# Fifteen residual transposes and six gate transposes of a two-block hybrid network moved from TensorE to the sync engine's DMA transpose

## The reference

```python
def hybrid_layer(x, norm_g, w_in, ...):
    u = rms_norm(x, norm_g)
    p = u @ w_in
    qk, v, o, z_a, ig, fg, xb, z_b = jnp.split(p, SPLIT_AT, axis=-1)
    ...
    xc = causal_dwconv(xb, lru_conv_w) + lru_conv_b
    y_b = rg_lru(xc.astype(f32), w_a, b_a, w_x, b_x, lam).astype(x.dtype) * jax.nn.silu(z_b)
    return x + jnp.concatenate([y_a, y_b], axis=-1) @ w_out

# second stack, each of four layers
        h = rms_norm_2(x, norm_g[i])
        z = h @ w_in
        ...
        branch = jnp.concatenate([mix_out, mem_out], axis=-1) * jax.nn.silu(gate)
        x = x + branch @ w_out[i]
```

## Time and profile before

| | us |
|---|---|
| runs of the kernel | 3285.24, 3285.38, 3286.81 (median 3285.38) |
| the profiled execution's own time | 3287.08 |
| its span | 3285.3 |
| PE busy | 3274.6 (100% of the span) |
| DVE busy | 2085.7 (63%) |
| ACT busy | 1748.3 (53%) |
| DMA engines' mean share | 58.1% for the load queue |

### The profile page before, as it was taken

One profiled execution on the slowest core, in us unless ns is written; L12 is line 12 of the kernel. 1 busy time (PEld: TensorE's weight loads), 2 busy tenths in 40 slices (PEclk: granted clock), 3 DMA queues, 4 the chain that ended last, 5 costly groups with the idle time before them and its releaser, 6 DMA issues.

```text
span 3285.3 us, 39697 instructions
## 1 busy us (share of the span) xinstructions
PE 3274.6 (100%) x15310; PEld 2728.1 (83%) x15310; DVE 2085.7 (63%) x2843; ACT 1748.3 (53%) x2322; POOL 173.9 (5%) x241
## 2 busy tenths in 40 slices
PE   9999999999999999999999999999999999999999
PEld 7888888888888888888888888888888888888887
DVE  6557655756757755657667665665565677757564
ACT  5554555546654455546655564455544555545563
POOL 2000000000000000000000000000000322200000
PEclk9999999999999999999999999999999999999999
DMA  8665666565565566565567665566656566665565
GB/s 273 211 200 172 207 190 188 192 191 175 182 185 179 187 198 194 185 200 174 184 197 223 186 209 181 170 178 187 193 181 190 168 181 180 193 207 186 183 199 173
DMA packets 352060, 626.77 MB, mean 191 GB/s; under 512 B 58428, under 2 KB 60804, under 8 KB 351488
## 3 DMA queue, kind: packets, MB, share of 16 engines
q1 hardware_dynamic: 339248, 590.49, 58.1%
q0 software_dynamic: 10336, 27.45, 2.7%
q10 hardware_dynamic: 2288, 6.30, 0.5%
HBM read 608.10 MB, written 6.62 MB: 187 GB/s over the span
## 4 chain that ended last, share of the span: by engine, by line
PE 98%; DVE 1%; DMA 0%; ACT 0%; issue 0%; SPq 0%; ACTq 0%
PE acc L1697 30%; PE acc L1699 30%; PE acc L1698 30%; PE tr L1784 1%; PE nm L1887 1%; PE tr L1766 1%; PE tr L1697 0%; PE tr L1699 0%; PE tr L1875 0%; PE tr L1698 0%; PE sc L1861 0%; DMA weights_raw<-in_w_mem_kv_dram 0%; PE sc L1852 0%; DVE weights_lo L1249 0%; PE tr L1887 0%; PE sc L1866 0%
## 5 line engine op out<-in xcount | busy, mean ns | idle before, releaser
L1249 DVE TENSOR_TENSOR weights_lo<-weights_raw,weights_hi 128x1024 fp32r<-128x1024 f32 x1103 | 1343.9, 1230 | 922.7 <-ACT weights_hi L933 918.7
L933 ACT ACTIVATE weights_hi<-weights_raw 128x1024 fp32r<-128x1024 f32 x1103 | 1160.5, 1058 | 1079.0 <-PE acc L1699 1034.0
L1697 PE MATMUL acc<-weights_hi,u_hi 128*128 128x512 f32 x3136 | 1238.2, 395 | 0.0
L1699 PE MATMUL acc<-weights_hi,u_lo 128*128 128x512 f32 x3136 | 1222.8, 390 | 0.0
L1698 PE MATMUL acc<-weights_lo,u_hi 128*128 128x512 f32 x3136 | 1221.6, 390 | 0.0
L1697 PEld LDWEIGHTS acc<-weights_hi,u_hi 128*128 128x128 f32 x3136 | 589.2, 188 | 123.8 <-issue 4.3
L1699 PEld LDWEIGHTS acc<-weights_hi,u_lo 128*128 128x128 f32 x3136 | 588.9, 188 | 123.6
L1698 PEld LDWEIGHTS acc<-weights_lo,u_hi 128*128 128x128 f32 x3136 | 589.4, 188 | 119.1
L1697 PE MATMUL acc<-weights_hi,y_hi 128*128 128x512 f32 x1280 | 502.6, 393 | 1.3 <-DVE y_lo L1253 1.2
L1699 PE MATMUL acc<-weights_hi,y_lo 128*128 128x512 f32 x1280 | 498.7, 390 | 0.0
L1698 PE MATMUL acc<-weights_lo,y_hi 128*128 128x512 f32 x1280 | 498.2, 389 | 0.0
(11 more groups left out here) (279 smaller groups left out, 1931.3 us busy)
## 6 DMA issues: line engine op xcount, KB each, us to landing
weights_raw<-in_w_in_dram SPq DMA_DIRECT2D x384, 512.0 KB, 3.7
weights_raw<-in_w_out_dram SPq DMA_DIRECT2D x256, 512.0 KB, 4.4
weights_raw<-in_a_w_in_dram SPq DMA_DIRECT2D x176, 512.0 KB, 4.2
weights_raw<-in_b_w_in_dram SPq DMA_DIRECT2D x112, 512.0 KB, 3.7
weights_raw<-in_c_w_in_dram SPq DMA_DIRECT2D x112, 512.0 KB, 4.3
weights_raw<-in_w_mem_kv_dram SPq DMA_DIRECT2D x63, 512.0 KB, 4.8
kv_scratch<-work ACTq DMA_DIRECT2D x8, 512.0 KB, 5.4
qk_tiles<-in_w_a_dram POOLq DMA_DIRECT2D x8, 512.0 KB, 4.4
```

Of the source, the lines that this page charges most:

```text
L933: SC_E.activation(WH[:, b % RING], RAW[:, b % RING], ACT.Copy).then_inc(sem("hi_done"), 1)
L1249: V.tensor_tensor(WL[:, b % RING], RAW[:, b % RING], WH[:, b % RING].bitcast(F32), ALU.subtract).then_inc(sem("lo_done"), 1)
L1697: T.matmul(dst, hi_l, hi_r, start=start, stop=False, **kw)
L1699: return T.matmul(dst, lo_l, hi_r, start=False, stop=stop, **kw)
```

## The change

Three edits and what goes with them.

First, in all five layer ends the tiles of columns 0 to 1535 (`x0`, `x1`, `x2`) go through `xbar`, and only `x3` stays with `tp`. The buffers are `u0` and `u1` in `work`; `x2` uses `u0` again and has its `join` four slots after `apart`, not five.

Second, in both hybrid layers the gate tile of groups p = 0, 1, 2 goes through `apart`, a `turn` and a new piece `zjoin` (ACT, two instructions), and `lrz` reads it from SBUF. `lrz` and `lry` stand three slots later than before. Group 3 keeps `cz`.

Third, every `xbar` now has its low part on DVE as a piece of its own, `low`, two slots after `join`. `apart` on a buffer waits for that `low`. One of the gMLP tiles gets a buffer of its own, `a0`.

```diff
-ISSUE, JOIN = 8, 5
+ISSUE, JOIN, LOW = 8, 5, 2
...
-    def xbar(slot, src, ready, dst, kt0, gain, buf):
+    def xbar(slot, src, ready, dst, kt0, gain, buf, join=JOIN):
 
         q = apart(slot, src, ready, buf)
-        return pl.piece(slot + JOIN, "join", dst=dst, kt0=kt0, gain=gain, at=q, buf=buf)
+        p = pl.piece(slot + join, "join", dst=dst, kt0=kt0, gain=gain, at=q, buf=buf)
+        pl.piece(slot + join + LOW, "low", at=p, buf=buf)
+        return p
...
         def lru_gate(p):
             zb = pl.chunk(("w_in", l, COL_ZB + CH * p, 0), "tok", "u", "zb")
-            pl.piece(pl.here() + 3, "cz", at=zb)
-            pl.piece(pl.here() + 5, "lrz", l=l, p=p)
-            lr.append(pl.piece(pl.here() + 7, "lry", l=l, p=p))
+            if p == 3:
+                pl.piece(pl.here() + 3, "cz", at=zb)
+                pl.piece(pl.here() + 5, "lrz", l=l, p=p)
+                lr.append(pl.piece(pl.here() + 7, "lry", l=l, p=p))
+            else:
+                q = apart(pl.here() + 1, "xt", ("zb_out", zb), "z")
+                pl.piece(pl.here() + 6, "zjoin", at=q, buf="z")
+                pl.piece(pl.here() + 8, "lrz", l=l, p=p, at=q)
+                lr.append(pl.piece(pl.here() + 10, "lry", l=l, p=p))
...
-            xt.append(tp(o + 1, "x%d" % j, ("ox_out", ox), "u", 4 * j,
-                         ("par2", FGN + 4 * j, 1) if l else ("par", NPAR + NG + 4 * j, 1)))
+            gain = ("par2", FGN + 4 * j, 1) if l else ("par", NPAR + NG + 4 * j, 1)
+            xt.append(tp(o + 1, "x3", ("ox_out", ox), "u", 12, gain) if j == 3 else
+                      xbar(o + 1, "x%d" % j, ("ox_out", ox), "u", 4 * j, gain, "u%d" % (j % 2), 4 if j == 2 else JOIN))
...
+                    elif k == "zjoin":
+                        act.wait_ge(sem("half_t_z"), 16 * (p.at.nth + 1))
+                        for t in range(2):
+                            to = joined("z")[:, :, P * t:P * t + P].bitcast(U16).rearrange("p f (k s) -> p s f k", s=2)
+                            i = SC_E.activation(to, turned("z")[:, 8 * t:8 * t + 8].rearrange("p (s f) k -> p s f k", s=2),
+                                                ACT.Copy)
+                        i.then_inc(sem("zj_out"), 1)
...
-                    elif k == "join":
+                    elif k == "low":
+                        p = p.at
                         hi, lo = ACTS[p.dst]
```

More of the change, by code:

```diff
@@ L453, in make_plan @@
                 ts.append(tp(pl.here() + 4, "o", ("sv_out", sv), "y", 8, None) if grp == 2 else
-                          xbar(pl.here() + 4, "o", ("sv_out", sv), "y", 4 * grp, None, "a"))
+                          xbar(pl.here() + 4, "o", ("sv_out", sv), "y", 4 * grp, None, "a" if grp else "a0"))
         else:
@@ L493, in make_plan @@
                 pl.piece(o, "sq", j=j, ready=("ox_out", ox))
-                xt.append(tp(o + 1, "x%d" % j, ("ox_out", ox), "u", 4 * j,
-                             ("par2", NG2 + 16 * (i + 1) + 4 * j, 1)))
+                gain = ("par2", NG2 + 16 * (i + 1) + 4 * j, 1)
+                xt.append(tp(o + 1, "x3", ("ox_out", ox), "u", 12, gain) if j == 3 else
+                          xbar(o + 1, "x%d" % j, ("ox_out", ox), "u", 4 * j, gain, "u%d" % (j % 2), 4 if j == 2 else JOIN))
     return pl.close()
@@ L890, in _ @@
                         wait(pool, "ox_out", p.last.get("ox"))
+                        wait(pool, "jn_lo", p.last.get("low"))
                         pool.dma_start(WS, A["a_w_s_2"][p.a].rearrange("h t s -> t h s")).then_inc(sem("ws_in"), 16)
@@ L982, in _ @@
                             act.wait_ge(sem("half_t_" + p.buf), 16 * p.nth)
-                        if p.buf == "q":
+                        if p.buf == "z":
+                            wait(act, "tp_pe", last["tp"])
+                            wait(act, "half_in", last["apart"])
+                            wait(act, "lrz_y", last.get("lrz"))
+                            wait(act, "mo_out", last["mo"])
+                        elif p.buf == "q":
                             wait(act, "mo_out", last.get("mo"))
@@ L987, in _ @@
                         else:
-                            wait(act, "jn_lo", last.get(("join", p.buf)))
+                            wait(act, "jn_lo", last.get(("low", p.buf)))
                         for t in range(2):
@@ L1076, in _ @@
                         wait(act, "cz_pe", last.get("cz"))
+                        wait(act, "half_in", last.get("apart"))
                         for t in range(2):
@@ L1174, in _ @@
                         SC_E.activation(SQB, SQB, ACT.Sqrt).then_inc(sem("lr_sq"), 1)
+                    elif k == "zjoin":
[5 more added lines that the diff above has]
+                        i.then_inc(sem("zj_out"), 1)
                     elif k == "lrz":
-                        wait(act, "cz_pe", p)
+                        if p.at:
+                            wait(act, "zj_out", last["zjoin"])
+                        else:
+                            wait(act, "cz_pe", last["cz"])
                         wait(act, "lw_pe", last["lgate"])
@@ L1179, in _ @@
                         for j in range(2):
-                            i = tanh(ZT[:, 2 * j:2 * j + 2], TR[:, j].rearrange("p (a b) -> p a b", b=256), scale=0.5)
+                            z = joined("z")[:, 2 * j:2 * j + 2] if p.at else TR[:, j].rearrange("p (a b) -> p a b", b=256)
+                            i = tanh(ZT[:, 2 * j:2 * j + 2], z, scale=0.5)
                         i.then_inc(sem("lrz_t"), 1)
@@ L1537, in _ @@
                             z = ZT[:, 2 * j:2 * j + 2]
[L1538 removed]
+                            raw = joined("z")[:, 2 * j:2 * j + 2] if p.at else TR[:, j].rearrange("p (a b) -> p a b", b=256)
+                            i = stt(z, z, 1.0, raw, ALU.add, ALU.mult)
                         step(i)
@@ L1562, in _ @@
                         wait(dve, "tp_pe", last["tp"])
+                        wait(dve, "half_in", last["apart"])
                         cs = slice(CH * p.j, CH * p.j + CH)
```

4 lines of the change are left out of this document (2 added, 2 removed).

## The result

The changed kernel takes 3320.25 us (median of 4 runs, 3316.20 to 3322.17); the kernel before, run beside it, 3285.68 (3285.24 to 3286.81). The ratio is 1.0103, with a 95% interval of 1.0090 to 1.0115: 34.6 us slower, where 38.5 were forecast. The profiled execution took 3321.58 us; its span, from the first to the last instruction, is 3319.8.

A forecast was written before the change was run, and what follows sets the result against it. PE, busy 3274.6 of 3285.3 us, was taken as the bound; 22.4 + 2.6 + 13.5 = 38.5 us slower, with PE's 18.9 given back inside it, made 3324 us, range 3290 to 3345.

The forecast's parts named there:

- PE gives back 0.90 us a group: On PE's list: 21 groups of eight transposes fewer, 0.90 us each, 18.9 us in all.
- Separate low parts at nothing: Low parts two slots later on DVE and buffer `a0`: zero, with +-2 us in all.
- ACT's rounding put behind `apart`, and its block late by 1.7: Recurrent groups 1 and 2: `apart` delays block 533's rounding, so PE waits 1.7 us to start that block.
- Group 0, two instances, 1.3 us each: Recurrent group 0: landing hidden, gate products 1.2 to 1.3 us later each, 2.6 us in all.
- Groups 1 and 2, four instances, 5.6 us each: Recurrent groups 1 and 2: late landing and the chain behind it end each instance 5.6 us later, 22.4 us.
- the landing: SP's transposes: landing 6.7 us after issue (5.4 to 8.3), with ACT waiting 3.0 us at `zjoin`.
- The 17.1 us of DVE's chain: Recurrent groups: from `lrz`'s tanh through DVE's list and convolution to PE's gate products takes 17.1 us.
- Layer ends, five, 2.7 us each: Layer ends: PE waits 0.3, 2.8 and 2.4 us against 2.7 given back; 2.7 net each, 13.5 us.
- SP's list: A transpose holds SP's list 4.60 us; later loads cost nothing, 0.5 us each place as upper end.
- (a): Rival: PE's relief stands alone, ACT and DVE catch up, no remainder late; 3266.5 us, chance 0.15 (or most of it).
- (b): Rival: only recurrent groups are late, layer ends hide all and gain 13.5 us; 3297 us, chance 0.10.
- (c): Rival: a transpose lands like a load, 4.4 us; 3303 us, chance 0.08 shared with a mild form of both waits.

The follow-up runs named there:

- e3: Changed kernel with all layer-end and gate tiles put back on PE, leaving only separate low parts and buffer `a0`: 3285.45 us.
- e11: Changed kernel, gate groups back on PE, transposes of `u0` and `u1` issued one slot earlier, `x3`'s transposes on PE one slot later: 3273.88 us.
- e1: Changed kernel with the recurrent gate groups put back on PE, layer ends left changed: 3295.5 us.
- e4: Changed kernel with gate groups back on PE and only `x0` and `x1` by SP, `x2` and `x3` on PE: 3285.73 us.
- e2: Changed kernel with all layer-end tiles put back on PE, gate tiles of groups 0 to 2 still by SP: 3312.1 us.
- e9: e2 with `warm(12)`, small matmuls nothing reads, on PE before the gate products: 3307.17 us.
- e12: e11 with the `join` of `x2` one slot later, five after its `apart`: 3275.28 us.
- e7: e2 with 24 calls of a small matmul nothing reads on PE before the gate products: 3322.62 us.
- e8: e2 without three quarters of the low part in `lry` for groups 0 to 2, so `y_lo` is incomplete: 3304.56 us.

## Why the prediction was right, and where it was not

The total came out near, and part of that is luck. By the traces, the mechanism as the prediction stated it costs 2.4 us in group 0, 19.0 in groups 1 and 2 and 4.5 at the layer ends, 25.9 in place of 38.5. The six stretches of half clock, which it had at nothing, add 9.4, and the one in the trace before takes off 1.7; of the 0.9 that is left to the 34.5 between the two spans, 0.6 is at the start of the kernel. Terms that were too large and one that was missing nearly cancelled.

**PE gives back 0.90 us a group: right**, within what can be read: 0.85 by the busy times of e3 and e11.

**Separate low parts at nothing: right.** e3, within 0.1% of none. The gate read from SBUF costs nothing either: the three products of `lrz` take 2.47 us (1623.98 to 1626.45), where they took 2.46.

**ACT's rounding put behind `apart`, and its block late by 1.7: right.** The rows have 1.55 of waiting.

**Group 0, two instances, 1.3 us each: right, but for the clock.** By PE's block starts, one against the other in the traces before and after, the instances cost 1.2 and 2.8. The second has the half clock behind its stop and the first hasn't; without its 1.6 it is 1.2 too.

**Groups 1 and 2, four instances, 5.6 us each: the sum is right by two errors.** The traces have 5.9, 5.8, 7.2 and 6.3, 25.2 in all against 22.4. 1.5 to 1.6 of each is half clock (four of four), so the stated chain cost 4.3, 4.3, 5.7 and 4.7. The step that was mis-sized is the landing: 6.7 was taken, the median of before; at the six new gate places five landings are 5.5 to 5.6, and one is 7.0. That one is the 5.7. The 4.7 has the 0.36 us in which ACT waits for a load behind the transpose. With a landing of 5.4, its lower bound, the prediction had 4.3, which is what stands there. ACT waited 0.8 for the landing at `zjoin`, not 3.0, and 2.3 where it took 7.0, because it stood 2.6 to 2.7 us just before that for the load issued right ahead of the transpose, a wait that the prediction hadn't seen and that cost nothing more. The 17.1 us of DVE's chain, from the tanh's end at about 1623.95 to 1641.08, are 17.1. The clock was missing altogether: PE's idle time was costed and what follows it was not.

**Layer ends, five, 2.7 us each: the mechanism right, the size too large.** Both stops are there in all five. For `x3` they are 2.05 to 2.1, forecast 2.4. For the remainder behind `x2`'s `join` they are 0.9 to 1.4, forecast 2.8, and the forecast 0.3 ahead of it is none. It is the landing again: 5.4 to 5.5 against 6.7, and ACT's wait at the `join` 3.0 to 4.1 against 5.5. By the traces the five cost 1.5, 0.6, 0.7, 0.8 and 0.9 without the clock, 4.5 in place of 13.5. The runs of e1 have 9.9, and the difference is mostly the clock. e1's profiled execution, the fastest of its runs, has 4.5 again without its two stretches of half clock, which add 3.2. Its median execution stands at a mean clock of 0.998, which by the estimate above takes three stretches or more. 4.5 and three times 1.6 are 9.3.

**SP's list.** 4.60 us for a transpose was taken; the median is 3.48. The loads behind it cost nothing that the traces show, but for the 0.36 us in one of the four instances; the prediction had nothing, with 0.5 at each place as the upper end.

**The prediction's own working** has small slips that don't change its answer. The transpose is issued 2.65 us after `apart` ends by its rows (387.34 to 389.99), not "some 2.4", and the walk uses 2.65. Its terms from the landing to the tanh add up to 9.0, not 9.2, and 1617.0 is 5.5 behind 1611.49, not 5.6. PE's longest wait in the trace before is the 2.9 us for the constants, not the 1.7.

**The rivals.** (a) decides at the remainder behind `apart` and `join`, and PE waits there. (b) had the layer ends gain 13.5 us; they cost 4.5 in the trace and 9.9 in e1's runs. Only with the moves of e11 do they gain, 11.9. (c) had a landing of 4.4, and its time, 3303, is 17 us too low, with nothing for the clock in it, like the forecast; the truth about the landing, 5.5 at the 21 new places in the median, lay halfway between the two. The Trainium skill has (c) as a rule ("Advanced Engine Details and Errata", section X-Bar Transpose (TRN2): as fast as regular DMAs). In the trace after it depends on which DMA is the regular one: 39 transposes took 5.3 to 7.4 us to land, 5.8 in the median, against medians of 3.8 to 5.2 for the 512 KB loads of weights, and 5.6 and 5.7 for the 512 KB stores from SBUF to DRAM. Taken as the load's 4.4, the rule gave too short a landing here.

**Signs that missed.** PE's busy time was to fall by about 15 us, and it fell by 3.6, 15.3 less than the 18.9 given back. The six stretches of half clock less the one before put back 7.7. Some 5 us more are in how a stop is counted: the last matmul ahead of it is shown busy for 0.39 us, though the next would start after 0.23, and the one behind it lasts longer (0.47 and 0.50 in place of 0.39), 0.2 to 0.27 a stop in the 26 stops. Two to three us stay open. And e4 was expected at 3278: the price of `x2`'s own transposes was taken from a layer end without `apart` ahead of them, though the prediction's own rule (DVE late by the work put in ahead) reaches them as well.

## What to carry to other kernels

A unit that saves 0.9 us on the busiest engine can be worth nothing if its replacement puts 1.9 us ahead of the next thing that engine needs and the lead there is 1.15: compare the two numbers at the place, before adding up the relief. Where a slow transfer is needed at a fixed point of an in-order list, first move its issue ahead of what waits in the issuing list, and its use one slot back; here either single slot was worth 18 us, nearly twice the part's whole loss. And cost a stop of the matmul engine with what comes behind it, too: a stop of 2.7 us could cost 1.6 us more. That a total comes out right does not show that its terms are: here it took the parts, place by place, to see it.

## What the runs showed of the hardware that was not expected

Behind stops of PE of 1.7 to 2.7 us the granted clock was at half for 3.4 us, though the engine had been busy before, and each such stretch cost 1.5 to 1.6 us. The length of the stop alone doesn't say when: in the trace of after, stops of 1.97 and 1.96 us before the gate products came out one at full and one at half clock, and in e2 a stop of 2.68 us (at 806.92) at full. The stop of 1.4 to 1.8 us between 2610 and 2660, which all the kernels have (in the one before at 2620), was followed by half clock in the traces of before, e9 and e12 and by full clock in all the others. Cheap matmuls in the stop kept the clock at 1.00 at all six places (e9), and were worth 4.9 us; where they outlasted the stop they cost 10.5 (e7). The spread of 4 to 6 us between the executions of after, e1, e2 and e8 goes with their mean granted clock.

A transpose of 512 KB from SBUF to SBUF landed in 5.3 us at the least and 5.8 in the median of the 39 after. It went by the place in the kernel: the six of the mLSTM took 6.2 to 7.3, and thirteen of the fifteen of the layer ends 5.3 to 6.0. The median of the kernel before (6.7), with none at these places, was no good measure for them.
